# Four more sums of squares as a high and a low half in two single-pass products

## The reference, cut to what matters

```python
def rmsnorm(x, g):
    xf = x.astype(jnp.float32)
    y = xf * lax.rsqrt(jnp.mean(xf * xf, axis=-1, keepdims=True) + EPS)
    return (y * g.astype(jnp.float32)).astype(x.dtype)
...
merged = jnp.concatenate([rmsnorm(a_out, g_out[:D_ATTN]), rmsnorm(b_out, ...), rmsnorm(c_out, ...)], axis=-1)
x = x + merged @ w_out
up = rmsnorm(x, g_ffn) @ w_up
```

## Time and profile before

| | |
|---|---|
| median of three runs | 1033.48 us |
| profiled execution, its own time | 1033.46 us |
| its span | 1031.6 us |
| TensorE matmuls, busy | 1020.8 us |
| VectorE, busy | 817.1 us |
| ScalarE, busy | 564.8 us |
| mean granted TensorE clock | 0.998 |

### The profile page before, as it was taken

How to read it: one execution, slowest core, us unless ns; L and a number is a source line. 1 busy time by engine, 2 the same in 40 slices (tenths; PEclk the granted TensorE clock), 3 DMA queues, 4 the chain that set the end, 5 groups by cost and what they waited for, 6 DMA issues and landing times.

```text
span 1031.6 us, 19728 instructions
## 1 busy us (share of the span) xinstructions
PE 1020.8 (99%) x7414; PEld 993.3 (96%) x7414; DVE 817.1 (79%) x1481; ACT 564.8 (55%) x1101; POOL 64.0 (6%) x161
## 2 busy tenths in 40 slices
PE   9999999999999999999999999999999999999996
PEld 8999988888999999999999999999999999999996
DVE  6854669997778889887887787787777898888974
ACT  7455445655554466555555655555556745446744
POOL 0000000000000011100010010101100000000023
PEclk9999999999999999999999999999999999999999
DMA  7311201022643312132131232222326974346364
GB/s 272 102 41 47 102 22 42 21 83 76 235 137 102 112 41 96 65 130 103 42 144 56 90 110 76 103 104 80 120 104 191 342 246 149 106 136 213 92 185 151
DMA packets 65038, 120.39 MB, mean 117 GB/s; under 512 B 5520, under 2 KB 48272, under 8 KB 64912
## 3 DMA queue, kind: packets, MB, share of 16 engines
q1 hardware_dynamic: 61120, 113.16, 32.3%
q10 hardware_dynamic: 3824, 5.96, 1.6%
HBM read 92.62 MB, written 27.53 MB: 116 GB/s over the span
## 4 chain that ended last, share of the span: by engine, by line
PE 95%; DVE 2%; ACT 1%; DMA 1%; issue 1%; SPq 0%; DVEq 0%; ACTq 0%
PE psum L3044 41%; PE psum L3118 12%; PE psum L2994 9%; PE psum L2774 8%; PE psum L3073 6%; PE psum L2841 3%; PE psum L3094 2%; PE psum L2843 2%; PE psum L3012 2%; PE psum L2842 2%; PE psum L2808 2%; PE psum L2925 2%; PE psum L2885 1%; PE psum L2935 1%; DMA raw<-in_w 1%
## 5 line engine op out<-in xcount | busy, mean ns | idle before, releaser
L3044 PE MATMUL psum<-diff,w_hi 128*128 128x258 f32 x588 | 116.5, 283 | 0.0
L3044 PE MATMUL psum<-h_hi,w_lo 128*128 128x258 f32 x336 | 95.2, 283 | 0.0
L3044 PE MATMUL psum<-h_hi,w_hi 128*128 128x258 f32 x336 | 95.0, 283 | 0.0
L3044 PE MATMUL psum<-diff,w_lo 128*128 128x258 f32 x336 | 94.9, 282 | 0.0
L3044 PE MATMUL psum<-h_lo,w_hi 128*128 128x258 f32 x336 | 94.8, 282 | 0.0
L3044 PE MATMUL psum<-h_hi,act_lo 128*128 128x258 f32 x336 | 94.7, 282 | 0.0
L3044 PE MATMUL psum<-h_lo,act_hi 128*128 128x258 f32 x336 | 94.5, 281 | 0.0
L3044 PE MATMUL psum<-h_hi,act_hi 128*128 128x258 f32 x336 | 94.5, 281 | 0.0
L3044 PEld LDWEIGHTS psum<-diff,w_hi 128*128 128x128 f32 x588 | 94.0, 190 | 0.0
L3044 PEld LDWEIGHTS psum<-h_hi,w_hi 128*128 128x128 f32 x336 | 63.8, 190 | 0.0
L3044 PEld LDWEIGHTS psum<-diff,w_lo 128*128 128x128 f32 x336 | 63.6, 189 | 0.0
(11 more groups left out here) (413 smaller groups left out, 3350.6 us busy)
## 6 DMA issues: line engine op xcount, KB each, us to landing
raw<-in_w SPq DMA_DIRECT2D x76, 512.0 KB, 4.1
act_d<-x_sb SPq DMA_DIRECT2D x10, 1032.0 KB, 5.2
zb<-act_d SPq DMA_DIRECT2D x28, 344.0 KB, 5.2
att<-in_w SPq DMA_DIRECT2D x15, 512.0 KB, 4.8
raw<-in_w SPq DMA_DIRECT2D x18, 384.0 KB, 3.6
act_d<-att SPq DMA_DIRECT2D x10, 516.0 KB, 2.7
x_sb<-in_x SPq DMA_DIRECT2D x8, 516.0 KB, 5.0
x_d<-x_sb ACTq DMA_DIRECT2D x12, 344.0 KB, 2.4
```

The source lines that it names most:

```text
L3044: ins = mm(bank[to, q], a, b, start=(fresh and k == p == 0), stop=(k == HALF - 1 and p == 2), skip_group_check=True)
```

## The change

Four more sums (C of tile 1, A of tile 2, C of tile 2, X of tile 0) get a high and a low half, in two new buffers that share the place of `pad_u`, which only the feed-forward block uses. Their products with the ones become two float32r products. `sum_hi` steps are put into ScalarE's program and `sum_lo` steps into VectorE's, and TensorE's four tasks wait for the low half in place of the sum. The float32 products of A of tile 1, C of tile 0, X of tiles 1 and 2 and those at the end stay as they are.

```diff
-SPLIT_SUMS = (("x", 0), ("x", 1), ("x", 2), ("B", 0), ("B", 1), ("A", 0))
+SPLIT_SUMS = (("x", 0), ("x", 1), ("x", 2), ("B", 0), ("B", 1), ("A", 0), ("C", 1), ("A", 2), ("C", 2), ("X", 0))
...
+        pad_u_base = nc.sbuf_base
         pad_u = sb("pad_u", [P, PADC])[:, :]
...
+        late_hi, late_lo = (nc.alloc_sbuf_tensor_at("late_sum_" + part, [P, TW], F32R, offset=(pad_u_base + 31) // 32 * 32 + o * TW * 4) for o, part in enumerate(("hi", "lo")))
+        for step, total in ((("C", 1), sq_c[:, 0, :]), (("A", 2), sq_a[:, 0, :]), (("C", 2), sq_c[:, 0, :]), (("X", 0), x2_sum[0])):
+            sum_parts[step] = total, late_hi[:, :], late_lo[:, :]
...
# ScalarE
             def sum_hi(which, t):
-                act.wait_ge(sq_sum_ready, SQ_STEPS.index((which, 0 if which == "B" else t)) + 1)
+                if which == "X":
+                    act.wait_ge(x2_added, KD - 1)
+                else:
+                    act.wait_ge(sq_sum_ready, SQ_STEPS.index((which, 0 if which == "B" else t)) + 1)
...
                 if o == 4:
+                    sum_hi("A", 2)
                     square_c(2)
                 if o == 3:
+                    sum_hi("C", 1)
                     square_a(2)
                     factor(("norm", "C", 1), rstd_c[1], 2 * P)
                 if o == 5:
                     merged_c(1)
                     factor(("norm", "A", 2), rstd_a[2], HG * P)
+                    sum_hi("C", 2)
...
+                if o == 10:
+                    sum_hi("X", 0)
...
# VectorE (ahead of out_evac(o) stand the low half of the weights and x2_add)
+                if o == 3:
+                    sum_lo("C", 1)
+                if o == 6:
+                    sum_lo("C", 2)
+                if o == 11:
+                    sum_lo("X", 0)
                 out_evac(o)
...
                 if o == 4:
+                    sum_lo("A", 2)
                     sq_tree("C", 2, 2, sq_c)
...
# TensorE, in task
-                    if which == "X":
+                    if which == "X" and t:
                         pe.wait_ge(x2_added, (KD - 1) * (t + 1))
```

## The result

The changed kernel took 1043.94 us (median of five runs, 1043.23 to 1045.85), the kernel before beside it 1034.63 us (1033.28 to 1035.78). The ratio is 1.0096, 95% interval [1.0084, 1.0107]: slower by some 10 us. The profiled execution is the slowest of the five, 1045.85 us with a span of 1043.9 us. The prediction started from a median of three runs, 1033.48 us, which lay at the low end of what this kernel does: in each group of runs here its median is 1034.1 to 1034.6 us, so ratios serve better than differences from 1033.48.

A forecast was written before the change was run, and what follows sets the result against it. TensorE bounds the kernel (matmuls fill 1020.8 of 1031.6 us). Terms +3.3, -0.26, -0.26, +3.7, -0.26 make +6.2, with restarts +6.4 to +6.5, on 1033.48: 1040.0 us; likeliest 1039.4 to 1040.8, 8 in 10 1038.8 to 1043.5.

The forecast's parts named there:

- C of tile 1: TensorE's product behind job 3: its low half comes late, making TensorE 3.3 us later, saving included; range 3.2 to 3.5.
- X of tile 0: TensorE's product behind job 11: its low half comes late, a stall of 3.7 us, bounds 3.6 to 4.1, less 0.26 saved.
- Direction and mechanism: Whole kernel slower, chance 0.93, through two TensorE waits ended by VectorE's subtractions, near 266 and 301 us.
- The savings: Each of the four products takes 0.31 us as a pair against 0.57 us in float32: 0.26 us each, 1.0 in all.
- the clock falls in a stall: Rival: TensorE's clock drops in one or both stalls, adding 1.7 us per fall; 1041.7 or 1043.4 us, chance 0.38.
- a clock that holds: Main case: both stalls occur and TensorE's clock stays at full level; 1040.0 us, chance 0.47.
- two falls: TensorE's clock drops in both stalls, giving 1043.4 us; one or two such drops together had chance 0.38.
- The price of 1.7 us each: Time lost per drop of TensorE's clock, taken above the middle between bounds of nothing and 2.5 us.
- Only one of the stalls: Rival: X's low half is made earlier and only C's stall is left, 1036.1 us; with half-size stalls, chance 0.08.
- faster: Rival: all pairs are ready when TensorE arrives and the four savings stand alone; 1032.4 us, chance 0.05.

The follow-up runs named there:

- no_x0: The changed kernel without the split of X of tile 0; 1038.87 us, ratio 1.0040 to the kernel before.
- no_c1: The changed kernel without the split of C of tile 1; 1039.38 us, ratio 1.0048 to the kernel before.
- warm: The changed kernel with 22 extra single-pass products ahead of each of the two waits; 1041.47 us, ratio 1.0067 to the kernel before.
- after: The changed kernel itself, first timing and profile; 1043.94 us, ratio 1.0096 to the kernel before.
- after_again: The changed kernel, unaltered, timed and profiled a second time; 1044.20 us, ratio 1.0095 to the kernel before.
- only_a2_c2: The changed kernel with only A and C of tile 2 split, the other two sums keeping float32 products; 1034.47 us, ratio 1.0000 to the kernel before.
- c1_early: The changed kernel with both helper steps of C of tile 1 and VectorE's subtraction of X of tile 0 moved earlier; 1036.27 us, ratio 1.0018.
- warm_half: The changed kernel with 11 extra single-pass products ahead of each of the two waits; 1041.63 us, ratio 1.0072 to the kernel before.
- in_time_2: The changed kernel with TensorE's C of tile 1 behind job 4, helper steps for it, A of tile 2 and X's subtraction earlier; 1033.97 us, ratio 0.9998.

## Why the prediction was wrong

**Direction and mechanism: right.** Two waits, at C of tile 1 and X of tile 0, none at A and C of tile 2, each ended by VectorE's subtraction.

**Size of the stalls: right.** C of tile 1: +3.3 us predicted (saving counted in), +3.25 measured in no_x0. X of tile 0: 3.7 less 0.26 predicted, +3.5 measured in no_c1. Together with the other two savings +6.2, against +6.07 in warm. Only the late landing of weights, 0.9 us in the profiled run, was in no term.

**The savings: right.** A pair costs 0.31 to 0.32 us, so 0.26 us below the float32 product. (The Trainium skill, FP8 and Floating Point Precision, TensorE Precision Notes, counts four passes for true float32. The prediction set each at 0.157 us, the pitch of a whole matmul, which gives a saving of 0.32; the product's turn of 0.57 us in the trace is measured and decides.)

**The step that failed: "the clock falls in a stall" was put below "a clock that holds", 0.38 to 0.47.** The argument against it, that both stalls lie between stretches of unbroken work, was wrong. In each profile with a wait of 3.4 us or more (after, after_again, no_c1, no_x0: six waits) the clock fell, six of six. The row for it stood in the trace of before: the clock had fallen 2.9 us after the end of the work, and both stalls were longer. This should have made two falls the forecast. The price of 1.7 us each, a choice between bounds in the prediction, was near: 1.6 us in after_again (9.29 - 6.07 = 3.2 for two), but some 2.4 us in the first profile (11.84 - 6.07 - 0.9 for the late weights = 4.9 for two). Two falls gave 1043.4 us; with the kernel's own median at 1034.1 to 1034.6 in place of 1033.48, the 9.9 us of that case would have led to 1044.0 to 1044.5, against medians of 1043.94 and 1044.20. The range ended at 1043.5 because it held two falls at one fixed price and nothing for the starting point. The Trainium skill (TensorE: Matmul & The Clock Gate, HAM oscillation) was on the right side: gaps between bursts, then a cold start. The traces agree on the fall; the work behind the gap started at the lower level in three of the six places, and in the other three the clock fell 0.7, 1.1 and 1.4 us later.

**The rivals.** "Only one of the stalls" and "faster" are out by the two waits. That the added work costs by itself, a rival of the experiments, is out by only_a2_c2 and by c1_early's stretch. The late landing of weights, 0.9 us in one profile, adds to C's wait and was not tested by itself.

## What to carry to other kernels

A faster form of an operation that needs one more step on another engine is worth its saving only if that step's result is there when the bound engine arrives: work out that instant from the timeline, by the queue of steps ahead of it, not from the helper's idle share. Where the bound engine is TensorE and the wait is as long as the time after which its clock fell elsewhere in the trace, count the fall with the wait: here it made 6 us into 9 to 10. A shorter wait is not safe for that reason: warm_half's clock fell behind 2.04 us, where the tail of the trace had shown 2.9. And a new step is not put early freely, even where its own product profits: what stands behind it comes later. In in_time_2 the steps of A of tile 2 ahead of the weights made scale, squares and bank some 1.6 us later, and TensorE waited for the bank.

## What the runs showed of the hardware

- The clock can fall after TensorE is back at work: 0.7 us (no_c1), 1.1 us (after_again) and 1.4 us (no_x0) behind the end of waits of 3.4 to 3.5 us. At half level a matmul's turn was 0.29 us (271.44 to 275.45 for 14 of them) and not 0.16.
- Waits of 1.71 us (warm_half) and 1.75 us (c1_early) did not bring the clock down, one of 2.04 us (warm_half) did; each was seen once.
- Useless products in a wait that exists anyway can shorten the time: with them the clock stayed at its full level and the kernel was 2.5 to 2.9 us faster, for two waits.
